# Delta rule heads: the transposed inverse by transposes and copies, the next pair's gates and sums of squares moved

## The reference, cut to what matters

```
q, k, v = silu(causal_conv(h @ w_in))              # per head; q, k l2-normalised
L = where(strict, (k*beta) @ k.T * decay, 0)
T = inverse(I + L)                                 # triangular_solve against the identity
v_corr = T @ (v*beta);  k_cumdecay = T @ (k*beta*exp(g))
attn_intra = where(tril, q @ k.T * decay, 0)
for each chunk:                                    # the state S
    v_new = v_corr - k_cumdecay @ S
    o = (q*exp(g)) @ S + attn_intra @ v_new
    S = S*exp(g_last) + (k*exp(g_last - g)).T @ v_new
o = rms_norm(o) * silu(z)
```

## Time and profile before

| what | value |
|---|---|
| median of three runs | 2865.66 us (2864.12 to 2866.37) |
| the profiled execution's own time | 2866.46 us |
| its span in the profile | 2864.7 us |
| mean granted TensorE clock | 0.983 |
| delta rule stage, from the first L1069 to the last L1268 | 293.6 to 679.8 us |

### The profile page before, as it was taken

How to read it: one execution, slowest core, us unless ns; L and a number is a source line. 1 busy time by engine, 2 the same in 40 slices (tenths; PEclk the granted TensorE clock), 3 DMA queues, 4 the chain that set the end, 5 groups by cost and what they waited for, 6 DMA issues and landing times.

```text
span 2864.7 us, 36987 instructions
## 1 busy us (share of the span) xinstructions
PE 2730.5 (95%) x14045; PEld 2338.0 (82%) x14045; DVE 1891.3 (66%) x3534; ACT 1193.5 (42%) x1927; POOL 537.9 (19%) x393
## 2 busy tenths in 40 slices
PE   8999999989998999999998999999999989999997
PEld 6787878878877999999997888888888547788886
DVE  3334765755555778786985889888887496444434
ACT  5445243233213454547994333333333445322322
POOL 0122220220000678772000112111110011000000
PEclk9999999999999999999999999999999999999999
DMA  4112101003562677775668889988984200232220
GB/s 163 52 52 89 59 30 45 30 30 116 216 226 90 226 288 281 279 248 200 258 243 297 338 328 352 339 329 333 347 320 145 83 30 21 90 103 103 88 103 30
DMA packets 141359, 501.19 MB, mean 175 GB/s; under 512 B 13400, under 2 KB 67072, under 8 KB 111616
## 3 DMA queue, kind: packets, MB, share of 16 engines
q1 hardware_dynamic: 122752, 364.60, 35.7%
q0 software_dynamic: 18432, 134.23, 11.9%
HBM read 450.53 MB, written 48.25 MB: 174 GB/s over the span
## 4 chain that ended last, share of the span: by engine, by line
PE 78%; DVE 11%; ACT 4%; DMA 3%; issue 2%; POOL 1%; SPq 0%; DVEq 0%; POOLq 0%; ACTq 0%
PE bank L247 21%; PE bank L249 21%; PE bank L248 21%; DVE xn L1534 2%; PE bank L2157 2%; DMA w_raw<-in_w_in_dram 2%; PE bank L1119 1%; PE bank L1109 1%; PE bank L1125 1%; PE bank L742 1%; DVE M L2947 1%; DVE whl L243 1%; DVE m L2943 1%; ACT whl L237 1%; PE bank L2745 1%
## 5 line engine op out<-in xcount | busy, mean ns | idle before, releaser
L247 PE MATMUL bank<-HH,uhl 128*128 128x384 f32 x1024 | 345.7, 338 | 1.9 <-POOL uhl L1660 1.9
L249 PE MATMUL bank<-HH,uhl 128*128 128x384 f32 x1024 | 342.8, 335 | 0.0
L248 PE MATMUL bank<-HL,uhl 128*128 128x384 f32 x1024 | 342.6, 335 | 0.0
L247 PE MATMUL bank<-vhl,awhl 128*128 128x512 f32 x768 | 301.1, 392 | 11.8 <-DVE awhl L2374 10.8
L249 PE MATMUL bank<-vhl,awhl 128*128 128x512 f32 x768 | 300.7, 392 | 0.0
L248 PE MATMUL bank<-vhl,awhl 128*128 128x512 f32 x768 | 300.7, 391 | 0.0
L1716 POOL DMA_INDIRECT gs<-in_uv_dram,idx x128 | 154.1, 1204 | 770.5 <-DVE x L1741 477.8
L2314 ACT ACTIVATE vhl<-vraw 128x1024 fp32r<-128x1024 f32 x128 | 135.7, 1061 | 321.8 <-PE bank L249 283.9
L1660 POOL TENSOR_TENSOR uhl<-ur,uhl 128x1024 fp32r<-128x1024 f32 x69 | 168.0, 2446 | 319.8 <-ACT uhl L1654 319.6
L243 DVE TENSOR_TENSOR whl<-w_raw,whl 128x2048 fp32r<-128x2048 f32 x49 | 114.6, 2339 | 160.3 <-ACT whl L237 160.3
L247 PE MATMUL bank<-HH,whl 128*128 128x512 f32 x528 | 213.7, 405 | 4.7 <-DVE whl L243 4.0
(11 more groups left out here) (421 smaller groups left out, 6241.3 us busy)
## 6 DMA issues: line engine op xcount, KB each, us to landing
ur<-in_peer_u_dram SPq DMA_DIRECT2D x128, 512.0 KB, 5.2
vraw<-in_peer_v_dram SPq DMA_DIRECT2D x128, 512.0 KB, 6.2
w_raw<-in_w_in_dram SPq DMA_DIRECT2D x36, 1024.0 KB, 5.0
xn<-in_ada_rows_dram SPq DMA_DIRECT2D x48, 512.0 KB, 4.7
g_scratch<-stg SPq DMA_DIRECT2D x12, 2048.0 KB, 7.9
gti<-g_scratch SPq DMA_DIRECT2D x16, 1536.0 KB, 11.8
wf_raw<-in_f_w_in_dram SPq DMA_DIRECT2D x22, 1024.0 KB, 4.8
act_scratch<-ag SPq DMA_DIRECT2D x96, 192.0 KB, 2.8
```

What stands on the lines that cost most here:

```text
L247: e.matmul(out, l[0], r[0], start=start, stop=False)
L248: e.matmul(out, l[0], r[1], start=False, stop=False)
L249: return e.matmul(out, l[1], r[0], start=False, stop=stop)
```

## The change

On PE, the product P^T X^T (L1125) of levels 0 to 4 is gone, with DVE's subtraction from `XT` (L1237) and POOL's two operations for XT's start. In its place every level transposes X on PE, in step 3+2l behind the head's P (four transposes per head), and ACT copies the result to `XT` before step 4+2l. The last level's product from XT, which was called "xt", is now called "x" and is subtracted from `XT` as before. ACT's first copy to XT of a head waits until the head two before it has read XT (V.onw), as POOL did.

The order of the next pair's pieces changes. The silus go from ACT's step 11 to steps 6 to 11 (`SILU`). The sums of squares go from steps 12 and 15 to 14 and 18 with their roots, two of the squares from step 14 to 16, and the scaling from 13 and 17 to 15 and 20. No transfer is moved.

```diff
@@ pe_gdn_head, 3 <= seg < 3 + 2 * LV @@
                 for tb in range(NT):
                     i = e.matmul(b[:, blk(tb)], B["LT"][:, tb, :], B["X"][:, tb, :], start=True, stop=True)
                 i.then_inc(*T.up("p", h, l))
-            else:
-                e.wait_ge(*(V.of("xt", h, l - 1) if l else G.of("XT", h)))
-                e.wait_ge(*V.of("p", h, l))
-                if l < LV - 1:
-                    b = R3.take("x", h, l)
...
-                    for tb in range(NT):
-                        i = e.matmul(b[:, blk(tb)], B["XT"][:, tb, :], PMs[f][:, tb, :], start=True, stop=True)
-                    i.then_inc(*T.up("x", h, l))
                 b = R3.take("xt", h, l)
...
                 for tb in range(NT):
-                    i = e.matmul(b[:, blk(tb)], PMs[f][:, tb, :], B["XT"][:, tb, :], start=True, stop=True)
+                    i = e.transpose(b[:, blk(tb)], B["X"][:, tb, :], ident)
                 i.then_inc(*T.up("xt", h, l))
+            else:
+                e.wait_ge(*A.of("xt", h, l))
+                e.wait_ge(*V.of("p", h, l))
+                b = R3.take("x", h, l)
...
+                for tb in range(NT):
+                    if l < LV - 1:
+                        i = e.matmul(b[:, blk(tb)], B["XT"][:, tb, :], PMs[f][:, tb, :], start=True, stop=True)
+                    else:
+                        i = e.matmul(b[:, blk(tb)], PMs[f][:, tb, :], B["XT"][:, tb, :], start=True, stop=True)
+                i.then_inc(*T.up("x", h, l))
@@ act_gdn_head @@
+        if 3 <= seg < 3 + 2 * LV and seg % 2:
+            l = (seg - 3) // 2
+            if l == 0 and h >= 2:
+                e.wait_ge(*V.of("onw", h - 2))
+            e.wait_ge(*T.of("xt", h, l))
+            e.activation(B["XT"][:, :, :], in4(R3.bank("xt", h, l)), ACT.Copy).then_inc(*R3.out(A, "xt", h, l))
@@ dve_gdn_head @@
-                if l < LV - 1:
-                    e.wait_ge(*T.of("x", h, l))
-                    e.tensor_tensor(B["X"][:, :, :], B["X"][:, :, :], in4(R3.bank("x", h, l)),
-                                    ALU.subtract).then_inc(*R3.out(V, "x", h, l))
-                e.wait_ge(*T.of("xt", h, l))
-                e.tensor_tensor(B["XT"][:, :, :], B["XT"][:, :, :], in4(R3.bank("xt", h, l)),
-                                ALU.subtract).then_inc(*R3.out(V, "xt", h, l))
+                X = B["X"] if l < LV - 1 else B["XT"]
+                e.wait_ge(*T.of("x", h, l))
+                e.tensor_tensor(X[:, :, :], X[:, :, :], in4(R3.bank("x", h, l)),
+                                ALU.subtract).then_inc(*R3.out(V, "x", h, l))
@@ pool_gdn_head @@
-        if seg == 1:
-            e.wait_ge(*A.of("lt", h))
...
-            e.tensor_tensor(B["XT"][:, :, :], B["LT"][:, :, :], cb("neg1T"), ALU.mult).then_inc(*G.up("xt0", h))
-            e.wait_ge(*G.of("xt0", h))
-            e.tensor_tensor(B["XT"][:, :, :], B["XT"][:, :, :], cb("ident"), ALU.add).then_inc(*G.up("XT", h))
@@ the order of the steps @@
+    SILU = {6: (0, 1), 7: (2,), 8: (3,), 9: (4,), 10: (5,), 11: (6, 7)}
@@ pe_gdn @@
-                    if g < 3 and seg in (12, 15):
-                        pe_gdn_ones(e, R3, g + 1, (2 if seg == 15 else 0) + f)
+                    if g < 3 and seg in (14, 18):
+                        pe_gdn_ones(e, R3, g + 1, (2 if seg == 18 else 0) + f)
@@ act_gdn @@
+                    if seg == 6 and g == 0:
+                        for i in (6, 7):
+                            act_gdn_silu(e, 0, i)
+                    for i in SILU.get(seg, ()):
+                        act_gdn_silu(e, g + 1, i)
                     if seg == 11:
-                        if g == 0:
-                            for i in (6, 7):
-                                act_gdn_silu(e, 0, i)
-                        for i in range(8):
-                            act_gdn_silu(e, g + 1, i)
                         for i in range(2):
                             act_gdn_square(e, g + 1, i)
                         e.preload_act_table_set(LN_SET)
...
-                        if seg in (12, 15):
-                            act_gdn_root(e, R3, g + 1, (2 if seg == 15 else 0) + f)
-                        if seg == 14:
+                        if seg in (14, 18):
+                            act_gdn_root(e, R3, g + 1, (2 if seg == 18 else 0) + f)
+                        if seg == 16:
                             act_gdn_square(e, g + 1, 2 + f)
@@ dve_gdn @@
-                        if seg in (13, 17):
-                            dve_gdn_normed(e, g + 1, (2 if seg == 17 else 0) + f)
+                        if seg in (15, 20):
+                            dve_gdn_normed(e, g + 1, (2 if seg == 20 else 0) + f)
```

More of the change, by code:

```diff
@@ L1110, in pe_gdn_head @@
                 i.then_inc(*T.up("p", h, l))
-            else:
-                e.wait_ge(*(V.of("xt", h, l - 1) if l else G.of("XT", h)))
-                e.wait_ge(*V.of("p", h, l))
-                if l < LV - 1:
-                    b = R3.take("x", h, l)
-                    for s in R3.empty("x", h, l):
-                        e.wait_ge(*s)
-                    for tb in range(NT):
-                        i = e.matmul(b[:, blk(tb)], B["XT"][:, tb, :], PMs[f][:, tb, :], start=True, stop=True)
-                    i.then_inc(*T.up("x", h, l))
                 b = R3.take("xt", h, l)
@@ L1124, in pe_gdn_head @@
                 for tb in range(NT):
-                    i = e.matmul(b[:, blk(tb)], PMs[f][:, tb, :], B["XT"][:, tb, :], start=True, stop=True)
+                    i = e.transpose(b[:, blk(tb)], B["X"][:, tb, :], ident)
                 i.then_inc(*T.up("xt", h, l))
+            else:
+                e.wait_ge(*A.of("xt", h, l))
+                e.wait_ge(*V.of("p", h, l))
+                b = R3.take("x", h, l)
+                for s in R3.empty("x", h, l):
+                    e.wait_ge(*s)
+                for tb in range(NT):
[4 more added lines that the diff above has]
+                i.then_inc(*T.up("x", h, l))
         if seg == 15:
@@ L1130, in pe_gdn_head @@
                 e.wait_ge(*s)
-            e.wait_ge(*V.of("xt", h, LV - 1))
+            e.wait_ge(*V.of("x", h, LV - 1))
             for tb in range(NT):
@@ L1225, in dve_gdn_head @@
             if seg % 2:
-                if l:
-                    e.wait_ge(*T.of("xt", h, l - 1))
                 e.wait_ge(*T.of("p", h, l))
@@ L1278, in pool_gdn_head @@
             e.tensor_tensor(B["X"][:, :, :], B["X"][:, :, :], cb("ident"), ALU.add).then_inc(*G.up("X", h))
-        if seg == 1:
-            e.wait_ge(*A.of("lt", h))
-            if h >= 2:
-                e.wait_ge(*V.of("onw", h - 2))
-            e.tensor_tensor(B["XT"][:, :, :], B["LT"][:, :, :], cb("neg1T"), ALU.mult).then_inc(*G.up("xt0", h))
-            e.wait_ge(*G.of("xt0", h))
-            e.tensor_tensor(B["XT"][:, :, :], B["XT"][:, :, :], cb("ident"), ALU.add).then_inc(*G.up("XT", h))
         if seg == 2:
```

## The result

The changed kernel takes 2825.36 us (median of four runs, 2821.03 to 2826.20) against 2865.20 us (median of four as well, 2864.12 to 2866.37) for the kernel before: a ratio of 0.986, with a 95% interval of 0.9847 to 0.9873. The forecast was 2824. The profiled execution took 2826.05 us with a span of 2824.2 us and a mean clock of 0.987. In the changed kernel the product for XT of the last level is L1127, and the other lines have moved: L1109 is still P, L1115 the transposes of X, L1125 X P, L1135 and L1141 `vc` and `kc`, L1188 ACT's copy to XT, L1235 the masks, L1240 the subtraction, L1271 the gating (before: L1268), L1154 to L1166 the recurrence.

What follows compares the result with a forecast made beforehand. PE, busy 95% of the span, was taken as the bound. Savings of 3.7 + 8.7 + 18.05 + 7.9 + 3.3 = 41.7 us from 2866.46 gave 2824.8, as a median 2824; range 2815 to 2841.

Steps and rivals of the forecast that it cites:

- The level: One level of pair 3 with no next pair's work between: 4.50 us in place of 5.60, ACT's copies in time.
- Rival (a): ACT's copies to XT set the pace: 0.6 us lost in each of 18 levels, 2835 us; chance 0.10.
- Levels 1 to 3: Levels with projections in pairs 0 to 2: 2.9 us saved a pair by shorter PE work, 8.7 in all.
- Level 0: First level of pairs 0 to 2: less POOL work brings DVE's masks earlier; saves 3.0, 5.35 and 6.5 us.
- Rival (b): DVE stays late in the first level because POOL's remaining work slows it: 9 us lost, 2833 us; chance 0.07.
- Pair 3: Last pair, without convolution: 3.2 us saved in its first level, clock still falling, and 3.7 in levels 1 to 5.
- Steps 11 to 14: Last levels of pairs 0 to 2: 11.0 us in place of 13.3, saving 2.3 a pair and 1.0 more in pair 0.
- The tail: From `vc` to the next pair's first matmul: sums partly hidden in the recurrence, 14.7 us, 1.1 saved a pair.
- rival (c): Transposes fail to keep PE's clock up, so steps without a projection run at 1.2 GHz: 2880 us; chance 0.05.
- rival (d): The merge after the stage waits for something else, so no saving reaches the end: 2866 us; chance 0.02.

Runs made afterwards that it cites:

- The order alone: New order of silus, squares, sums and scalings with the old products for XT, against the kernel before: 2852.65 us, ratio 0.9953 to 0.9980.
- The inverse alone: Transposes of X copied to XT, with the old order of silus, squares, sums and scalings, against the kernel before: 2848.09 us, ratio 0.9927 to 0.9964.

## Why the prediction was right

**The level.** Predicted 4.50, measured 4.66. The groups of 0.89 and 0.44 were right; the handovers were short. The prediction called X of h0 ready 0.15 ahead of the next P, with 0.04 from PE to DVE and nothing from DVE to PE. By the records it takes 0.21 + 0.69 + 0.14 = 1.04 where 0.89 is to be had, so P is 0.15 late. The 0.04 was a reading from the chain of waits, whose pieces end later than a sum of the records' starts: by the starts, the copy at 663.64 comes 0.28 behind its group (662.47 + 0.89 = 663.36). ACT's copy of h1 had its margin of 0.25 shrink to 0.09, less than such a handover: the hole of 0.07 in X P fits that, though no run took it away. Rival (a) priced late copies at 0.6 a level, and a tenth of it is there. What the copies can cost showed elsewhere: with the old order, they hold ACT's queue back, and the squares behind them, 16 us in steps 11 to 14.

**Levels 1 to 3.** Predicted 2.9 a pair, measured 2.9. The projections cover the waits, and what remains is that each head makes four transposes (0.44) in place of four products (0.89).

**Level 0.** Predicted 3.0, 5.35 and 6.5, measured 2.94, 5.51 and 6.61. The mechanism was right as well: POOL stands beside one of the convolution's operations and no longer beside three, so DVE is no longer late, and the clock does not fall. The run with POOL's work kept puts a number on it: 2.1 us that the masks of pair 1 are late, where the prediction took 1.75. Rival (b) would have kept the stand of 3.03; it is 0.05. With POOL's work kept, level 0 of the three pairs still saves 9.2 of the 15.1 us, with a full clock in pairs 1 and 2; the removed POOL operations are worth 5.9 there, the rest is PE's shorter path and the clock. So the clock is no part of what POOL's absence gives in pairs 1 and 2: with the transposes in the gap the stand is only 1.79, and it holds.

**Pair 3.** Predicted 3.2 for level 0 and 3.7 for levels 1 to 5, measured 5.1 and 2.0 by the start of level 1's P (599.09), 7.05 together against 6.9. The stand was 2.65 and not 2.9, and the slow stretch fell later, over the end of level 0 and the start of level 1; its whole price, by the profile in which it is missing, is 1.4 and not the 2.5 assumed. That the two parts miss by 1.9 and 1.7 in opposite directions and leave 7.05 against 6.9 is luck.

**Steps 11 to 14.** Predicted 2.3 a pair and 1.0 more in pair 0, measured 2.4 and 1.0 more. The hole forecast in step 14 is 0.17 and not 0.4 (the transposes of pair 1 are through at 466.63 + 0.44 = 467.07, X P starts at 467.24). The order alone gives nearly the same, 11.13 in place of 11.09, so this term belongs to the order: what the inverse saves in level 4 it pays in level 5, which makes transposes besides its product. The inverse alone would have lost there; the prediction counted both edits together and did not have to know.

**The tail, the mis-sized term.** Predicted: the sums go into the recurrence, which takes 9.2 in place of 8.54, 1.1 saved a pair. Measured: by the records' starts 15.68 before and 15.74 after, nothing saved; the recurrence (476.2 to 486.6) takes 10.4. The prediction gave both bounds, "if wholly added, nothing", and took a value between. The holes in the recurrence are there, but they are not where the sums go: with the sums computed twice, the tail grows by the whole 1.72, and both holds stay. The sums must sit between two half-steps, on the path; what DVE does meanwhile (two decay operations before them, two scalings behind) is also on the path. The order alone has the same tail, 15.74, so the term is the order's and the inverse has no part in it. This accounts for 3.5 of the 41.65 - 38.95 = 2.7 us by which the stage's saving was less than forecast, and the other terms give 0.8 back. By these parts the profiled execution would have come to 2866.46 - 38.95 = 2827.5 us; it came to 2826.05, because the part behind the stage took 1.5 less, which no term had and which lies within its spread. So the sum of the terms was 2.7 too good, chance gave 1.5 back, and that the forecast lies as near as 1.4 to the median is in part luck.

**The clock, rival (c).** It was given 0.05. No window of steps 11 to 14 is below 1.00, nor one of pair 3's levels once the stretch behind the stand is over; transposes are a fifth of them. The single row that the prediction set against the rule, 0.97 granted after transposes alone, was a true sign of what 100 transposes show.

**The merge, rival (d).** Refuted by the first row of the stage's end: ACT's L237 moved by the full 39.0.

## What to carry to other kernels

Before placing work on an engine with free time, look at what its queue holds back for the others. The copies to XT cost PE at most the hole of 0.07 us a level, but ahead of eight silus and two squares they held these back by 2.7 us, and PE stood for the squares: 16 us lost in three pairs, the fall of the clock included. Work that is put between the half-steps of a recurrence is added whole unless it sits in the very wait; first spread the other engines' operations that stand ahead of the update, here worth 1.4 us a pair for two changed step numbers. And when two edits come together, measure each alone: here they gave 14.7 and 9.1 us apart and 39.0 together.

## What was not expected of the hardware

Transposes alone hold TensorE's clock: 100 of them, 10.92 us, with 1.00 granted throughout and 0.109 us each. After pair 3's stand of 2.65 us the clock fell to half in four profiles and not in a fifth, at the same place of the same code; where it fell it cost 1.4 us. After 1.44 (two profiles) and 1.79 (pairs 1 and 2 with POOL's work kept) it did not fall, and after 2.15 in the tail, with the sums in step 19, it fell in all three pairs. The way from PE over one operation of DVE and back to PE costs 0.35 us beside the operation itself (0.21 in, 0.14 out, by the records' starts), which is more than the margins that a schedule with groups of 0.89 and operations of 0.69 leaves.
